# The output projection, its norms and the first up units merged into one phase by token blocks, and a reversed distance table

## The reference

```python
for l in range(DEPTH):
    h = rms_norm(x, norm_mix_pre[l])
    z = h @ w_in[l]
    # group A: latent attention, 4 heads; group B: dilated windows with a bias by distance, 4 heads
    # group C: grouped-query attention, 8 heads
    mix = jnp.concatenate([oa, ob, oc], axis=-1) @ w_out[l]
    x = x + rms_norm(mix, norm_mix_post[l])
    h = rms_norm(x, norm_ffn_pre[l])
    x = x + rms_norm(conv_gated_mlp(h, w_up[l], conv_w[l], conv_b[l], w_down[l]), norm_ffn_post[l])
```

## Time and profile before

| | us |
|---|---|
| median of 3 runs | 4004.22 (4004.12 to 4004.69) |
| the profiled execution | 4003.96 |
| its span, first to last instruction | 4002.2 |
| mean granted PE clock, share of full | 0.969 |

### The profile page before, as it was taken

The page is one execution under the profiler, slowest core; times in us unless marked ns, Lnnn a source line. Parts: engine busy times, 40 slices in busy tenths (PEclk is TensorE's granted clock), DMA queues, the critical chain, the costliest instruction groups (busy, mean ns, idle before and its releaser), DMA issues. The chain is left out here.

```text
span 4002.2 us, 51121 instructions
## 1 busy us (share of the span) xinstructions
PE 3779.0 (94%) x18821; PEld 3088.3 (77%) x18821; DVE 1903.0 (48%) x2890; ACT 1578.5 (39%) x2485; POOL 1186.0 (30%) x852
## 2 busy tenths in 40 slices
PE   6899999999799999999869999999988999999997
PEld 5687788778488888888657867877757888888884
DVE  5104867961734433344451257689345433344336
ACT  3323777972422112221342357689433112221223
POOL 2224433421512122121432244334224122121224
PEclk8998999999899999999989989999999999999998
DMA  5322221101311111111224123211031111111113
GB/s 177 118 74 68 67 63 31 37 22 55 109 38 39 35 42 37 37 42 31 74 84 131 60 63 80 53 31 31 26 112 51 34 42 37 37 42 31 42 31 132
DMA packets 194300, 234.43 MB, mean 59 GB/s; under 512 B 13759, under 2 KB 157669, under 8 KB 193573
## 3 DMA queue, kind: packets, MB, share of 16 engines
q1 hardware_dynamic: 194125, 232.18, 19.1%
HBM read 178.05 MB, written 58.29 MB: 59 GB/s over the span
## 5 line engine op out<-in xcount | busy, mean ns | idle before, releaser
L213 PE MATMUL ps<-hh,wh 128*128 128x512 f32 (+1 forms) x3264 | 1179.8, 361 | 116.5 <-DVE wl L506 44.1
L214 PE MATMUL ps<-hl,wh 128*128 128x512 f32 (+1 forms) x3264 | 1165.0, 357 | 0.0
L215 PE MATMUL ps<-hh,wl 128*128 128x512 f32 (+1 forms) x3264 | 1162.7, 356 | 0.0
L213 PEld LDWEIGHTS ps<-hh,wh 128*128 128x128 f32 x3264 | 623.3, 191 | 216.7 <-issue 86.1
L214 PEld LDWEIGHTS ps<-hl,wh 128*128 128x128 f32 x3264 | 623.3, 191 | 92.3 <-issue 5.8
L215 PEld LDWEIGHTS ps<-hh,wl 128*128 128x128 f32 x3264 | 622.5, 191 | 88.7
L1886 POOL TENSOR_TENSOR wl<-raw,wh 128x1024 fp32r<-128x1024 f32 x128 | 306.3, 2400 | 1278.7 <-ACT wh L1815 1278.7
L1922 DVE SCALAR_TENSOR_TENSOR cb<-ps,params,cb 128x1023 f32<-128x1023 f32 (+1 forms) x176 | 147.3, 878 | 895.9 <-ACT cb L1824 895.9
L1557 DVE TENSOR_REDUCE mx<-ps 128x1 f32<-128x512 f32 x512 | 352.5, 689 | 177.8 <-PE ps L1357 107.6
L1451 ACT ACTIVATE ph<-ps 128x512 fp32r<-128x512 f32 (+1 forms) x576 | 330.2, 573 | 183.5 <-PE ps L1325 176.8
L1824 ACT ACTIVATE cb<-ps,params 128x1280 f32<-128x1280 f32 x88 | 125.1, 1421 | 666.2 <-PE ps L215 642.2
(11 more groups left out here) (169 smaller groups left out, 5071.1 us busy)
## 6 DMA issues: line engine op xcount, KB each, us to landing
raw<-in_w_up SPq DMA_DIRECT2D x88, 512.0 KB, 3.9
heads<-stage SPq DMA_DIRECT2D x38, 640.0 KB, 3.3
raw<-in_w_down SPq DMA_DIRECT2D x44, 512.0 KB, 3.5
xo<-residual SPq DMA_DIRECT2D x32, 640.0 KB, 6.4
rq<-heads SPq DMA_DIRECT2D x56, 320.0 KB, 4.9
raw<-in_w_in SPq DMA_DIRECT2D x32, 512.0 KB, 4.5
rk<-heads SPq DMA_DIRECT2D x32, 320.0 KB, 4.3
residual<-y SPq DMA_DIRECT2D x8, 1024.0 KB, 5.0
```

What stands on the lines that cost most here:

```text
L213: pe.matmul(out, wh, xh, start=(k == 0), stop=False)
L214: pe.matmul(out, wh, xl, start=False, stop=False)
L215: last = pe.matmul(out, wl, xh, start=False, stop=(k == len(pairs) - 1))
```

## The change

- output_projection and the first add_normed of a layer become one phase, project_and_normalise. The output units run by token blocks: all eight over block 0, then block 1, then block 2. All eight split weights stay in SBUF. The sums, roots, norms, residual, high and low parts of a block are issued among the units of the next blocks, and the two up units follow block by block.
- The squares are added up on DVE, so that each sum over partitions is one product with ones. DVE multiplies by the root directly from its PSUM bank, and the second norm overwrites y; it waits until that block is stored.
- The residual is loaded and stored per chunk and token block.
- ACT loads its table at the start of this phase.
- The distance tables in DRAM go: a head's table is read as 128 overlapping windows of one line, which gives the keys in reversed order. The score products use a reversed identity (flip_r), the maxima stream the keys backwards and take one table product per block.
- perm_a becomes the same tile as perm_c.

The encoder calls project_and_normalise(nc, c, L) in place of the two. The diff, cut to its core, has less indentation in the new function, whose streams stand in the order SP, PE, ACT, POOL, DVE. In it, products(out, n, b, chunks) issues the three products per chunk of unit n and block b; take(n, b) is evacuate and square; new_sums and new_roots are as sums and roots, for the new squares (new_added, m_acc[1], bank R2); add_new_squares adds them as add_square does; low_weight(n) is POOL's low part of a weight.

```diff
-                for h in range(H_B):
-                    sp.dma_start(c.s_lines[h], bass.AP(tensor=c.s_line.tensor, offset=h * N_DIST, ap=[[0, P], [1, N_DIST]])).then_inc(stored, 16)
                 for t0, w in BLOCKS:
...
-                            src = bass.AP(tensor=c.s_lines.tensor, offset=(h - 4) * P * N_DIST + P - 1 + i * GW // 2,
-                                          ap=[[N_DIST - 1, P], [1, GW // 2]])
+                            src = bass.AP(tensor=c.s_line.tensor, offset=(h - 4) * N_DIST + i * GW // 2,
+                                          ap=[[1, P], [1, GW // 2]])
...
-                        prods += [(c.ident_r[:], c.gh[h % 2][:, x0:x0 + w]), (c.ident_r[:], c.gl[h % 2][:, x0:x0 + w])]
+                        prods += [(c.flip_r[:], c.gh[h % 2][:, x0:x0 + w]), (c.flip_r[:], c.gl[h % 2][:, x0:x0 + w])]
...
-                    mm = pe.matmul(out, c.q1[h % 3][0:r, qt * P:qt * P + P], c.k1[kv(h)][0:r, k0:k0 + w], start=True, stop=kind(h) != "B")
+                    keys = c.k1[kv(h)][0:r, k0:k0 + w]
                     if kind(h) == "B":
-                        for kk in range(w // P):
-                            x0 = qt * P - (k0 + kk * P) + 896
-                            mm = pe.matmul(out[:, kk * P:kk * P + P], c.gh[h % 2][:, x0:x0 + P], c.ident_r[:],
-                                           start=False, stop=(kk == w // P - 1))
+                        keys = keys[:, ::-1]
+                    mm = pe.matmul(out, c.q1[h % 3][0:r, qt * P:qt * P + P], keys, start=True, stop=kind(h) != "B")
+                    if kind(h) == "B":
+                        x0 = 1024 + qt * P - k0 - w
+                        mm = pe.matmul(out, c.ident_r[:], c.gh[h % 2][:, x0:x0 + w], start=False, stop=True)
...
+    ADD_ON_DVE = (2, 4, 6)
+    OUT_BANKS = (1, 2, 4, 5)
+    R1, R2 = 6, 7
+    def y_chunk(b, k):
+        if b == 2:
+            return c.my[0][:].rearrange("p k t -> p (k t)")[:, 256 * k:256 * k + 256]
+        return c.my[b][:, k, :]
+    def x_chunk(b, k):
+        if b == 0:
+            return c.mx_ring[k][:] if k < 5 else c.my[1][:, k, :]
+        if b == 1:
+            return c.my[0][:, 4 + k, :] if k < 4 else c.mx_ring[k - 4][:]
+        half = slice(256 * (k % 2), 256 * (k % 2) + 256)
+        return c.mx_ring[4][:, half] if k < 2 else c.my[0][:, 4 + (k - 2) // 2, half]
...
+    def load_raw(n, src):
+        sp.wait_ge(w_lo, n - 1)
+        sp.dma_start(c.raw[n % 2][:], src).then_inc(raw_arrived[n % 2], 16)
+    def load_x(b, k):
+        t0, w = BLOCKS[b]
+        sp.dma_start(x_chunk(b, k), c.s_x[:, k, t0:t0 + w]).then_inc(x_in[b], 16)
+    def store(b):
+        t0, w = BLOCKS[b]
+        for k in range(KC):
+            wait_added(sp, b, k)
+            sp.dma_start(c.s_x[:, k, t0:t0 + w], y_chunk(b, k)).then_inc(stored, 16)
     for n in range(2, KC):
+        load_raw(n, out_unit(c, L, n))
+    for k in range(KC):
+        load_x(0, k)
+    for i in range(2):
+        load_raw(KC + i, up_unit(c, L, 0, i))
+    store(0)
+    sp.wait_ge(new_added, KC - 1)
+    for k in range(4, KC):
+        load_x(1, k)
+    for k in range(2):
+        load_x(2, k)
+    wait_low(sp, lo_pool, lo_dve, 0)
+    sp.wait_ge(stored, 16 * KC)
+    for k in range(4):
+        load_x(1, k)
+    store(1)
+    sp.wait_ge(new_added, KC - 1 + 2)
+    for k in range(2, KC):
+        load_x(2, k)
+    for i in range(2):
+        load_raw(KC + 2 + i, up_unit(c, L, 0, 2 + i))
+    store(2)
+    for i in range(2):
+        sp.wait_ge(raw_arrived[i], 16 * 5)
+    sp.wait_ge(stored, 16 * 3 * KC)
...
+    def out(n, b):
+        x = KC * b + n
+        if b == 0:
+            pe.wait_ge(w_lo, n + 1)
+        if x >= 4:
+            pe.wait_ge(evacuated, x - 3)
+            pe.wait_ge(squared, x - 3)
+        products(bank(c, OUT_BANKS[x % 4], BLOCKS[b][1]), n, b, range(KC)).then_inc(unit_done, 1)
+    def sums(b):
+        w = BLOCKS[b][1]
+        pe.wait_ge(acc_added, (KC - 1) * (b + 1))
+        if b >= 1:
+            pe.wait_ge(scaled, KC * b)
+        pe.matmul(bank(c, R1, w), c.ones[:], c.m_acc[0][:, 0:w], start=True, stop=True).then_inc(summed, 1)
...
+    def up(u, b, between=None):
+        o = bank(c, 3 * u + b, BLOCKS[b][1])
+        if b == 0:
+            pe.wait_ge(w_lo, KC + u + 1)
+        products(o, KC + u, b, range(4))
+        if between:
+            between()
+        products(o, KC + u, b, range(4, KC)).then_inc(up_done, 1)
     for n in range(KC):
+        out(n, 0)
+    for n in range(KC):
+        out(n, 1)
+        if n == 0:
+            sums(0)
+        if n == 3:
+            new_sums(0)
+    for n in range(KC):
+        out(n, 2)
+        if n == 0:
+            sums(1)
+        if n == 5:
+            new_sums(1)
+    wait_low(pe, lo_pool, lo_dve, 0)
+    up(0, 0, lambda: sums(2))
+    up(1, 0)
+    wait_low(pe, lo_pool, lo_dve, 1)
+    pe.wait_ge(evacuated, 3 * KC)
+    pe.wait_ge(squared, 3 * KC)
+    up(0, 1, lambda: new_sums(2))
+    up(1, 1)
+    wait_low(pe, lo_pool, lo_dve, 2)
+    up(0, 2)
+    up(1, 2)
...
+    def split(n):
+        if n >= 2:
+            act.wait_ge(raw_arrived[n % 2], 16 * (n // 2))
+        if n >= KC:
+            act.wait_ge(unit_done, 2 * KC + n - KC + 1)
+        act.activation(weight(n)[0][:], c.raw[n % 2][:], ACT.Copy).then_inc(w_hi, 1)
+    def evacuate(n, b):
+        x = KC * b + n
+        w = BLOCKS[b][1]
+        src = bank(c, OUT_BANKS[x % 4], w)
+        act.wait_ge(unit_done, x + 1)
+        if b == 1 and n >= 5:
+            act.wait_ge(new_added, KC - 1)
+        act.activation(y_chunk(b, n), src, ACT.Copy).then_inc(evacuated, 1)
...
+    def square(n, b):
+        x = KC * b + n
+        w = BLOCKS[b][1]
+        act.wait_ge(unit_done, x + 1)
         if n == 0:
+            if b >= 1:
+                act.wait_ge(summed, b)
+            dst = c.m_acc[0][:, 0:w]
+        else:
+            if (KC - 1) * b + max(n - 2, 0) > 0:
+                act.wait_ge(acc_added, (KC - 1) * b + max(n - 2, 0))
+            dst = c.m_sq[n % 2][:, 0:w]
+        act.activation(dst, bank(c, OUT_BANKS[x % 4], w), ACT.Square).then_inc(squared, 1)
...
+    def roots(b):
+        r = bank(c, R1, BLOCKS[b][1])
+        act.wait_ge(summed, b + 1)
+        act.activation(r, r, ACT.Ln, scale=1.0 / D, bias=c.eps[:]).then_inc(logged, 1)
+        act.wait_ge(logged, b + 1)
+        act.activation(r, r, ACT.Exp, scale=-0.5).then_inc(root, 1)
+    def new_squares(b, chunks):
+        w = BLOCKS[b][1]
+        for k in chunks:
+            wait_added(act, b, k)
+            if k == 0 and b >= 1:
+                act.wait_ge(new_summed, b)
+            dst = c.m_acc[1][:, 0:w] if k == 0 else x_chunk(b, k)
+            act.activation(dst, y_chunk(b, k), ACT.Square).then_inc(new_squared, 1)
...
+    for n in range(3):
+        split(n)
+    take(0, 0)
+    split(3)
+    split(4)
+    take(1, 0)
+    split(5)
+    split(6)
+    take(2, 0)
+    split(7)
+    for n in range(3, KC):
+        take(n, 0)
+    evacuate(0, 1)
+    roots(0)
+    square(0, 1)
+    new_squares(0, range(2))
+    take(1, 1)
+    new_squares(0, range(2, 6))
+    take(2, 1)
+    new_squares(0, range(6, KC))
+    take(3, 1)
+    new_roots(0)
+    high(0, range(4))
+    take(4, 1)
+    high(0, range(4, KC))
+    for n in range(5, KC):
+        take(n, 1)
+    wait_low(act, lo_pool, lo_dve, 0)
+    evacuate(0, 2)
+    roots(1)
+    square(0, 2)
+    take(1, 2)
+    new_squares(1, range(2))
+    take(2, 2)
+    new_squares(1, range(2, 4))
+    take(3, 2)
+    new_squares(1, range(4, 6))
+    take(4, 2)
+    split(KC)
+    new_squares(1, range(6, KC))
+    take(5, 2)
+    split(KC + 1)
+    new_roots(1)
+    take(6, 2)
+    high(1, range(3))
+    take(7, 2)
+    high(1, range(3, 6))
+    roots(2)
+    high(1, range(6, KC))
+    new_squares(2, range(KC))
+    new_roots(2)
+    high(2, range(KC))
...
+    def add(b):
+        pool.wait_ge(x_in[b], 16 * KC)
+        for k in range(KC):
+            if k not in ADD_ON_DVE:
+                pool.wait_ge(scaled, KC * b + k + 1)
+                pool.tensor_tensor(y_chunk(b, k), y_chunk(b, k), x_chunk(b, k), ALU.add).then_inc(added_pool, 1)
+    def low(b):
+        t0, w = BLOCKS[b]
+        for k in range(KC):
+            if k not in LOW_ON_DVE:
+                pool.wait_ge(hi_done, KC * b + k + 1)
+                pool.tensor_tensor(c.hl[:, k, t0:t0 + w], y_chunk(b, k), c.hh[:, k, t0:t0 + w].bitcast(F32),
+                                   ALU.subtract).then_inc(lo_pool, 1)
     for n in range(KC):
+        low_weight(n)
+    add(0)
+    low(0)
+    add(1)
+    low_weight(KC)
+    low_weight(KC + 1)
+    low(1)
+    add(2)
+    low(2)
...
+    def add_square(n, b):
+        w = BLOCKS[b][1]
+        acc = c.m_acc[0][:, 0:w]
+        dve.wait_ge(squared, KC * b + n + 1)
+        if n >= 2:
+            dve.wait_ge(acc_added, (KC - 1) * b + n - 1)
+        dve.tensor_tensor(acc, acc, c.m_sq[n % 2][:, 0:w], ALU.add).then_inc(acc_added, 1)
```

(128 more changed lines are left out.)

76 lines of the change are left out of this document (43 added, 33 removed).

## The result

| | median us | lowest to highest | ratio to before |
|---|---|---|---|
| before, beside it | 4004.45 | 4004.12 to 4006.48 | |
| after | 3896.08 | 3887.53 to 3896.13 | 0.9723 [0.9706, 0.974] |
| forecast | 3874.0 | 3860 to 3905 | |

The change saves 108.4 us; 130.4 were forecast. The measured 3896.08 us lies in the stated range of 3860 to 3905, but outside the 3862 to 3884 that the forecast kept for itself. The profiled execution took 3896.13 us, its span is 3894.3 us, 107.9 less than before.

What follows compares the result with a forecast made beforehand. PE, 94% busy, was taken as the bound. Savings of 96.4 us (merged phase, two layers), 28.6 (max scores) and 5.4 (table) sum to 130.4, giving 3874 us; range 3860 to 3905, own range 3862 to 3884.

Steps and rivals of the forecast that it cites:

- The first rival: Group B heads: reversed keys stream at half rate, or PE's products don't set the time; 3903 to 3906 us, 13%.
- the second rival: Merged phase: norm instructions still take 1.31 and 1.02 us, 8 us of stalls per layer instead of 2.5; 3885 us, 15%.
- Input phase: Four 1 MB table writes leave it; its end moves from 55.6 to 50.2 us, saving 5.4 us.
- Max scores: Group B heads: one 512-column table product replaces four of 128; steps fall from 2.30 to 2.09 us, saving 28.6 us.
- Norms: Merged phase, DVE: a norm instruction with its factor in PSUM takes 0.69 us, not 1.31 or 1.02.
- Table load: ACT's load moves to the merged phase's start, ahead of the first split; 1.28 us that nothing hides.
- Weights, stores: Merged phase: weight supply at 4 us per weight hides behind 5.44 us units; store waits are covered, the last perhaps 1 to 2 us.
- The slower rival: Merged phase: the second norm's waits for stores, three per layer, outgrow their cover; 3925 us, 3%, of which 2 slower than before.
- Stalls: PE's waits in the merged phase: 2.5 us per layer, between 0 and 12, including 1 us at new_sums(1).
- Start at half clock: Merged phase: the first block of 24 products takes 7.4 us, a later one 5.44, as PE begins at half clock.
- The other waits: Merged phase, PE waits besides new_sums(1): 0.5 and 1 us of the 2.5 us of stalls per layer.
- MLP entry: Same barrier and first waits, raw weights loaded ahead as before; no change in time.

Runs made afterwards that it cites:

- forward_keys: The changed kernel with group B's max scores reading keys forward, so the maxima belong to other keys; 3894.55 us.
- psum_no_load: psum_acc without the ACT table load written at the start of project_and_normalise; 3875.6 us.
- psum_acc: The changed kernel with square accumulators (first norm block 2, second norm block 1) in PSUM banks, the last add writing SBUF; 3877.45 us.
- low_stub: The changed kernel with POOL's low parts of the two up units computed for one of eight row blocks only, accumulators still in SBUF; 3881.92 us.

## Why the prediction was right, and where 22 us went

The time fell inside the range, and the forecast mechanism is the one seen; a term was mis-sized. The range owes some of this to luck: it reaches to 3905 us only for the rival of keys at half rate, which did not happen, and 3896 lies between the second rival's 3885 and that rival's 3903. The prediction allows stalls of 0 to 12 us in one place and of 0 to 6 in its own range; PE's waits inside the phase are 7.9 us per layer. By its own steps, in the two profiled spans (130.4 forecast, 107.9 measured):

- **Input phase: right.** The wait for the residual's stores is 2.5 us instead of 10.4, and PE's first product of the next phase comes 6.2 us earlier (71.01 to 64.79), 5.4 forecast.
- **Max scores: right.** Attention's last work ended at 877.60 us before and 857.55 after; less the 6.2, 13.85 us in layer one, and the same stretch gives 14.3 in layer two (803.2 to 789.0 us from the first product of the layer to PE's last of attention), for 14.3 forecast. A step of a B head is 2.07 us (first scores product at 504.73 and 506.80), 2.09 forecast, and PE stays full with DVE at 113 of 160 us. The first rival fell with the key product's 0.23 us and with forward_keys.
- **Norms: right.** 0.74 us at 128x512 where the earlier trace rows have 1.31 and 1.02: the second rival's price didn't come. The Trainium skill (SBUF — State Buffer, Who interferes with whom) says that a DVE instruction with one SBUF input doesn't contend with GpSimd. The trace agrees: the two norms at 968.10 take 1.40 us together, though the first of them lies inside a POOL add of 967.66 to 969.33.
- **Table load: right in size and place**, 1.28 us on the path. That it need not be there at all was not looked for, nor that the first products took longer in most of the starts behind it (psum_no_load).
- **Weights, stores: right.** PE has no other idle time in block 0; of the six sums' waits only those of new_sums have a size, 0.16, 7.04 and 0.72 us. The norm's wait for stores never shows: stores land in 1.7 to 3.6 us, under the 3.4 to 7.2 of the earlier trace rows. The slower rival had nothing to stand on.
- **Stalls: the step that failed.** "new_sums(1) is due at 993.1 and waits 1 us for DVE's last add." It waited 7.04 and 6.84, over the 5 us that the prediction itself named as the sign of a wrong step, and half clock behind it took another 2.3 us (10 us at 0.77; the same stretch up to sums(2) takes 11.61 us in layer one and 9.46 in psum_acc, 2.15 less). That is 6.0 + 2.3 = 8.3 us per layer of the 9.7 by which the phase is longer than forecast. Start at half clock is a further 1.1: 16.05 us at 0.81 lose 3.0, the forecast had 7.4 - 5.44 = 2.0. The other waits, 0.9 us where 1.5 were forecast, give 0.6 back, so about 0.9 per layer stays unassigned.
- **MLP entry: right**, 5.82 us for 5.78. MLP itself was taken as unchanged, and each, with the norms behind it, took 1.5 and 2.0 us longer, from its first product to that of layer two or to the end (953.6 for 952.1, 953.7 for 951.7). Over the eight traces that have the merged phase, this same code takes 951.3 to 953.9 and 950.8 to 954.0 us, so 1.5 and 2.0 are no more than runs differ. The mean clock (0.9796 for 0.9804, 0.9850 for 0.9860) accounts for 0.7 and 1.0 of them; the rest stays open.

2 x 9.7 for the phase, 3.4 for the MLPs and 0.5 for the scores, less 0.8 for the input phase, come to 22.5, and the spans are 22.5 us short of the forecast.

Why the step failed: with 1 us of wait for the last add the walk left DVE's adds their lone 0.4 to 0.7 us, and took POOL's low parts as hidden since PE didn't wait for them. The second rival did name the adds and low parts, with their operands in SBUF, as something that POOL and DVE still share, but priced only slower norms by it. I applied the rule on SBUF inputs to the norms, where it spoke for the change, and not to the adds of squares in the same stretch, which have two SBUF inputs and speak against it. psum_acc moves only the accumulators, one input of each add and the output of all but the last, and gets 18.6 us; low_stub changes just the other party and gets 14. Both came within 8 us of the forecast, psum_acc within 3.5: its span fell by 127.8 us of 130.4, PE's wait is 1.18 us where 1 was forecast, and the phase with its table load takes 149.2 us for 147.7. That the collision is the cause of the long wait is shown, as lowering it from either side shortens the wait and the adds; how the lost time splits between waiting for POOL and the order it forces on ACT is only read from the trace.

## What to carry to other kernels

When work is merged so that engines overlap for the first time, price each DVE instruction of the overlap by its operands' places and by what POOL does in those microseconds, and not from a row where it ran alone. A chain of adds whose end PE waits for is a candidate for PSUM, with its last add alone writing SBUF, where POOL works from SBUF in the same microseconds and banks are free. And look at what table an activation phase inherits before you load one.
